# Five of eight sums over channels: added chunk by chunk on GpSimd, then one product with ones

## What is computed

```python
h = rms_norm_2(x, mix_norm)                    # mean of squares over the 1024 channels
a, g = split(h @ w_in + b_in)                  # conformer_conv
h = a * sigmoid(g)
h = causal depthwise convolution of 31 taps + conv_b
h = silu(layer_norm(h, ln_g, ln_b))            # mean, then mean of squares of the difference
x = x + (h @ w_out + b_out)
x = x + square(relu(rms_norm_2(x, mlp_norm) @ w1)) @ w2     # again a mean of squares
```

## Time and profile before

| | |
|---|---|
| median of three runs | 3348.47 us |
| the profiled execution: its own time | 3347.38 us |
| its span (first to last instruction) | 3345.6 us |
| PE busy | 3172.8 us, 95% |
| DVE busy | 2033.8 us, 61% |
| ACT busy | 1068.4 us, 32% |
| POOL busy | 315.4 us, 9% |
| share of PE in the chain that ended last | 78% |

### The profile page before, as it was taken

One profiled execution on the slowest core, in us unless ns is written; L12 is line 12 of the kernel. 1 busy time (PEld: TensorE's weight loads), 2 busy tenths in 40 slices (PEclk: granted clock), 3 DMA queues, 4 the chain that ended last, 5 costly groups with the idle time before them and its releaser, 6 DMA issues.

```text
span 3345.6 us, 52078 instructions
## 1 busy us (share of the span) xinstructions
PE 3172.8 (95%) x22004; PEld 2531.4 (76%) x22004; DVE 2033.8 (61%) x3235; ACT 1068.4 (32%) x1526; POOL 315.4 (9%) x307
## 2 busy tenths in 40 slices
PE   8999999788988888999999999999999999999999
PEld 7777786577766666778888888877746888778887
DVE  4665454577777775535444454448979987654445
ACT  5222334444444442222111111123244333433332
POOL 0222342000000000400000000000000000000000
PEclk9999999799999998999999999999999999999999
DMA  3342666234344433421111111111101222223222
GB/s 144 120 138 63 219 217 197 72 80 105 85 104 99 98 65 136 152 95 38 51 51 39 50 51 51 51 38 38 38 25 51 89 100 101 83 81 126 96 93 76
DMA packets 93527, 301.86 MB, mean 90 GB/s; under 512 B 10352, under 2 KB 38640, under 8 KB 70768
## 3 DMA queue, kind: packets, MB, share of 16 engines
q1 hardware_dynamic: 79104, 246.63, 23.7%
q0 software_dynamic: 14192, 51.91, 4.6%
HBM read 241.35 MB, written 57.15 MB: 89 GB/s over the span
## 4 chain that ended last, share of the span: by engine, by line
PE 78%; DVE 11%; DMA 3%; issue 3%; ACT 2%; POOL 2%; SPq 1%; DVEq 0%; ACTq 0%; POOLq 0%
PE ps L2416 26%; PE ps L308 20%; PE ps L503 6%; PE ps L1755 3%; PE ps L2239 2%; PE ps L2559 2%; DMA Dn<-nbs 2%; PE ps L2074 1%; DVE Yh L2586 1%; PE ps L475 1%; PE ps L1423 1%; PE ps L1766 1%; PE ps L1778 1%; PE ps L1019 1%; PE ps L2436 1%
## 5 line engine op out<-in xcount | busy, mean ns | idle before, releaser
L2416 PE MATMUL ps<-Hh,whi 128*128 128x512 f32 x1600 | 498.0, 393 | 0.6 <-DVE wlo L288 0.6
L284 ACT ACTIVATE whi<-raw 128x2048 fp32r<-128x2048 f32 x139 | 265.7, 1912 | 590.7 <-PE ps L308 290.6
L288 DVE TENSOR_TENSOR wlo<-raw,whi 128x2048 fp32r<-128x2048 f32 x139 | 319.0, 2295 | 136.8 <-ACT whi L284 136.6
L2416 PEld LDWEIGHTS ps<-Hh,whi 128*128 128x128 f32 x1600 | 300.2, 188 | 69.3 <-issue 5.7
L2416 PE MATMUL ps<-Hh,wlo 128*128 128x512 f32 x800 | 311.4, 389 | 0.0
L308 PE MATMUL ps<-Hlo,whi 128*128 128x512 f32 x656 | 202.0, 389 | 0.0
L308 PE MATMUL ps<-Hhi,wlo 128*128 128x512 f32 x656 | 202.0, 389 | 0.0
L308 PE MATMUL ps<-Hhi,whi 128*128 128x512 f32 x656 | 202.0, 389 | 0.0
L2416 PE MATMUL ps<-aHh,whi 128*128 128x512 f32 x512 | 199.4, 389 | 0.1
L2416 PE MATMUL ps<-aLh,whi 128*128 128x512 f32 x512 | 199.3, 389 | 0.0
L2416 PE MATMUL ps<-aHh,wlo 128*128 128x512 f32 x512 | 199.3, 389 | 0.0
(11 more groups left out here) (385 smaller groups left out, 6175.9 us busy)
## 6 DMA issues: line engine op xcount, KB each, us to landing
raw<-in_panels SPq DMA_DIRECT2D x139, 1024.0 KB, 4.8
rwf<-F POOLq DMA_DIRECT2D x16, 1280.0 KB, 6.8
L<-rwf SPq DMA_DIRECT2D x16, 1024.0 KB, 4.9
L<-rwf SPq DMA_DIRECT2D x64, 256.0 KB, 4.1
Dn<-nbs SPq DMA_DIRECT2D x128, 128.0 KB, 5.7
gts<-so POOLq DMA_DIRECT2D x16, 512.0 KB, 3.5
gl<-gts SPq DMA_DIRECT2D x32, 256.0 KB, 3.4
rwt<-so POOLq DMA_DIRECT2D x15, 512.0 KB, 3.0
```

The lines of the kernel that those rows point to most:

```text
L284: e.activation(whi[i % 2][:, :], raw_of(i)[:, :], AF.Copy).then_inc(*a_hi.up(i))
L288: e.tensor_tensor(wlo[i % 2][:, :], raw_of(i)[:, :], whi[i % 2][:, :].bitcast(F32), OP.subtract).then_inc(*v_lo.up(i))
L2416: m = e.matmul(ap, W[wi][:, kc, n0:n0 + 128], mov[mi][:, kc, :], start=x == 0 and q == 0, stop=x == len(kcs) - 1 and q == 2)
```

## The change

Five sums are made another way: `sum2` of both halves, and `mu`, `var` and `sum3` of half 1. The new `added_pool` adds the eight chunks on POOL, seven additions of 128 x 512 into `sgt[h]` (a buffer that is otherwise the sigmoid's); then PE makes one product of ones with `sgt[h]` (`added_pe`, or a line in `first_pe`). The other three sums (`mu`, `var`, `sum3` of half 0) stay as they are. ACT's squares wait for POOL's addition where they waited for PE's product. In `first_pe` the product stands behind the eight chunks and before the products of panel `ci1`. In `down_dve`, block 10, DVE now makes the low part of chunk n-1 after adding chunk n; before, it made chunks 0 and 1 there and the others behind the block. ACT makes all eight chunks of half 0 before the cast of panel `ci1`; before, that cast stood behind the fifth.

```diff
--- before.py
+++ after.py
@@ -2276,12 +2276,12 @@
 
     def down_dve(e, p, t, v, b):
         for n in range(8):
-            if b == 10 and n == 6:
-                first_lo_dve(e, 0, range(2))
             for h in range(2):
                 e.wait_ge(*t.by("x", b, n, h))
                 e.tensor_tensor(xT[:, n, hs(h)], ring.bank("down", p, n, h), xT[:, n, hs(h)],
                                 OP.add).then_inc(*v.up("x", b, n, h))
+            if b == 10 and n:
+                first_lo_dve(e, 0, range(n - 1, n))
         if b < 10:
             panels_after(panel_dve, e, p)
 
@@ -2426,6 +2426,25 @@
             made.append((ap, W, n0, key))
         return made
 
+    def added_pool(e, key, h, src_by, src, free=None):
+
+        for kc in range(1, 8):
+            if kc == 1:
+                if free:
+                    e.wait_ge(*free)
+                e.wait_ge(*src_by(0))
+            else:
+                e.wait_ge(*g_e.by(key, h, kc - 1))
+            e.wait_ge(*src_by(kc))
+            e.tensor_tensor(sgt[h], src(0) if kc == 1 else sgt[h], src(kc), OP.add).then_inc(*g_e.up(key, h, kc))
+
+    def added_pe(e, key, h):
+        ap, waits = ring.take((key, h), (v_e, key, h))
+        for w in waits:
+            e.wait_ge(*w)
+        e.wait_ge(*g_e.by(key, h, 7))
+        e.matmul(ap, ones, sgt[h], start=True, stop=True).then_inc(*t_e.up(key, h, 7))
+
     def sums_pe(e, key, src_by, src, kcs=range(8)):
         if kcs[0] == 0:
             ap, waits = ring.take(key, (v_e, *key))
@@ -2441,7 +2460,7 @@
         for kc in kcs:
             e.wait_ge(*v_ff.by("x", 10, kc, h))
             if kc >= 2:
-                e.wait_ge(*t_e.by("sum2", h, kc - 2))
+                e.wait_ge(*g_e.by("sum2", h, max(kc - 2, 1)))
             e.activation(tq[h][kc % 2], xT[:, kc, hs(h)], AF.Square).then_inc(*a_e.up("sq2", h, kc))
             if kc == 0:
                 e.wait_ge(*t_ff.by("u", 21, 1))
@@ -2474,8 +2493,6 @@
             e.wait_ge(*w)
         outs = outs_pe(e, [((x, h, 0), (v_e, x, h, 0), weights(p, 8), n0) for x, n0 in (("a", 0), ("gate", 128))])
         for kc in range(8):
-            e.wait_ge(*a_e.by("sq2", h, kc))
-            e.matmul(ap, ones, tq[h][kc % 2], start=kc == 0, stop=kc == 7).then_inc(*t_e.up("sum2", h, kc))
             e.wait_ge(*v_e.by("lo2", h, kc))
             for o, W, n0, key in outs:
                 for q, (wi, mi) in enumerate(THREE):
@@ -2483,6 +2500,8 @@
                                  stop=kc == 7 and q == 2)
                 if kc == 7:
                     m.then_inc(*t_e.up(*key))
+        e.wait_ge(*g_e.by("sum2", h, 7))
+        e.matmul(ap, ones, sgt[h], start=True, stop=True).then_inc(*t_e.up("sum2", h, 7))
         if h == 0:
             panel_pe(e, p + 1)
         for x, n0 in (("a", 0), ("gate", 128)):
@@ -2666,7 +2685,7 @@
                 for k in range(2):
                     half_pe(e, ("co", h, n + k), (v_e, "co", h, n + k), weights(i, 8), 128 * k, Gh[h], range(8))
             last_use[i] = (t_e, ("co", h, n + 1))
-            if n:
+            if n and h == 0:
                 sums_pe(e, ("sum3", h), lambda kc: a_e.by("sq3", h, kc), lambda kc: tl_[kc % 2], (n - 2, n - 1))
 
     def co_dve(e, h, n):
@@ -2680,7 +2699,7 @@
     def last_act(e, h, n):
         e.wait_ge(*v_e.by("co", h, n))
         if n >= 2:
-            e.wait_ge(*t_e.by("sum3", h, n - 2))
+            e.wait_ge(*(g_e.by("sum3", 1, max(n - 2, 1)) if h else t_e.by("sum3", 0, n - 2)))
         e.activation(tl_[n % 2], xT[:, n, hs(h)], AF.Square).then_inc(*a_e.up("sq3", h, n))
 
     def last_pe(e, h):
@@ -2726,7 +2745,7 @@
             for k in range(2):
                 half_pe(e, ("m", h, b, k), (a_e, "r", h, b, k), W, 128 * k, Gh[h], range(8))
                 if h == 0 and b == 15 and k == 0:
-                    last_pe(e, 1)
+                    added_pe(e, "sum3", 1)
         last_use[p] = (t_e, ("m", h, b, 1))
 
     def up_act(e, h, b):
@@ -2788,9 +2807,9 @@
             if b:
                 back_pe(e, 0, b - 1)
             if b == 12:
-                mean_pe(e, 1)
+                added_pe(e, "mu", 1)
             if b == 13:
-                var_pe(e, 1)
+                added_pe(e, "var", 1)
             if b == 14:
                 co_pe(e, 1)
         back_pe(e, 0, 15)
@@ -2804,9 +2823,8 @@
         done["B"] = 0
         for i, u in enumerate(uA):
             e.memset(u[:, 0:30], 0.0).then_inc(*v_e.up("pad", i))
-        first_lo_dve(e, 0, range(2, 5))
+        first_lo_dve(e, 0, range(7, 8))
         panels_after(panel_dve, e, UIX["fd10"])
-        first_lo_dve(e, 0, range(5, 8))
         mean_dve(e, ("sum2", 0), 0, 1e-6)
         first_lo_dve(e, 1, range(4))
         recip_dve(e, ("sum2", 0), 0)
@@ -2908,9 +2926,8 @@
             back_dve(e, 1, 15, n)
 
     def late_act(e):
-        first_act(e, 0, range(5))
+        first_act(e, 0)
         panels_after(panel_act, e, UIX["fd10"])
-        first_act(e, 0, range(5, 8))
         root_act(e, ("sum2", 0), 0)
         first_act(e, 1)
         root_act(e, ("sum2", 1), 1)
@@ -2981,8 +2998,13 @@
                 panels_after(panel_act, e, UIX[f"md{b - 1}'"])
 
     def late_pool(e):
+        for h in range(2):
+            added_pool(e, "sum2", h, lambda kc: a_e.by("sq2", h, kc), lambda kc: tq[h][kc % 2])
         for ch in range(8):
             tail_pool(e, ch)
+        added_pool(e, "mu", 1, lambda ch: v_e.by("taps", 1, ch), lambda ch: Yh[1][:, ch, :], last_tap(1, 7))
+        added_pool(e, "var", 1, lambda ch: a_e.by("sqy", 1, ch), lambda ch: sqy(1, ch), t_e.by("mu", 1, 7))
+        added_pool(e, "sum3", 1, lambda n: a_e.by("sq3", 1, n), lambda n: tl_[n % 2], t_e.by("var", 1, 7))
 
     def late_sp(e):
         panels_sp(e, UIX["mg0"] + 7, UIX["mu4'"])
```

## The result

The changed kernel takes 3326.32 us (median of four runs, 3316.74 to 3328.50) against 3350.61 for the kernel before on the same chips (four runs, 3344.15 to 3353.14). The ratio is 0.9925 with a 95% interval of 0.990 to 0.9949: 25 us faster, between 17 and 34. The forecast was 3321.9, a gain of 25.5; the median lies 4.4 us above it, and the two medians are 24.3 apart. The profiled execution has a span of 3324.4 us, 21.2 less than before.

The account below looks back on a forecast made before the run. PE, busy 95% of the span, was taken as the bound. A gross 30.5 us less waits of 0.7, 2.5 and 1.8 gave 25.5, so 3347.38 became 3321.9 us; range 3317 to 3327, 8 in 10 for 3313 to 3332.

Parts of the forecast that it names:

- The gross, 30.5 us: PE's work saved at the five sums: 12.4 us for both `sum2`, 12.0 for `mu` and `var`, 6.1 for `sum3`.
- POOL is never late: At `sum2`, `mu` and `sum3` POOL's additions, 1.27 us alone, 1.8 where DVE is dense, cost PE 0.
- Term 1: Behind `sum2` of half 1, PE waits about 0.7 us (0 to 1) for a bank that DVE reads.
- Term 2: Behind `mu`, POOL's `var` additions delay DVE's subtractions and panel `md12`'s low part; PE waits 2.5 us (0 to 5.9).
- Term 3: Behind `var`, PE reaches `co_pe` before DVE frees its bank and waits 1.8 us (0 to 2.5).
- POOL costs DVE more than one panel: Rival: the 21 additions of `sum2` and `mu` also block low parts and taps; gain 14 us, 3333; chance 0.15.
- The gross did not come through unreduced: Denies the rival that none of the three waits appears and the full 30.5 us comes: 3316.9 us; chance 0.20.
- The swallowed stage: Rival: the DVE-led stage of 2497 to 2578 swallows `sum2`'s 12.4 - 0.7 us: 3333.6; chance 0.06.
- Slower through long additions: Rival: POOL's addition far longer than 1.27 us, PE waits at the sums; slower from 4.4 us on; chance 0.02.
- the estimate by turns of 1.09: At panel `md12`: five POOL turns each cost DVE 1.09 us; low part 13.3 us after `mean_dve`, PE waits 2.5.
- the one by the full addition: At panel `md12`: by the exclusive port rule each turn costs DVE the full 1.27 us; PE waits 3.3.

Follow-up runs that it names:

- version 8: Changed kernel plus the edits of experiment 4, experiment 6 and experiment 7, and `sum2`'s product of ones of half 1 ahead of the last chunk's products: 3316.59 us.
- experiment 4: Changed kernel, but POOL waits for the last of the eight squares before its first addition of `var`: 3324.03 us, ratio 0.9941.
- experiment 7: On top of experiment 4, DVE reads the first two chunks of `back_pe(0, 13)` before making the first co panel's low part: 3316.66 us, ratio 0.991.
- experiment 1: Changed kernel with `var` of half 1 put back to eight products of ones on PE, no POOL additions for it: 3325.46 us, ratio 0.994.
- experiment 3: Kernel before, plus POOL's seven additions of `var`, half 1, whose sum nobody reads: 3354.17 us, ratio 1.0019.
- experiment 6: On top of experiment 4, DVE takes the mean of `var` ahead of the low part of panel `md13`: 3326.08 us, ratio 0.9935.
- experiment 2: Changed kernel with only the two sums `sum2` on POOL; `mu`, `var` and `sum3` of half 1 as before: 3342.03 us, ratio 0.9984.
- experiment 5: Changed kernel with the first half's low parts and ACT's cast of panel `ci1` back in their old order: 3331.00 us, ratio 0.9947.

## Why the prediction was right, point by point

- **The gross, 30.5 us: right.** From the ledger with the waits taken out: `sum2` 57.71 - 45.33 = 12.4 (version 8, without the bank's wait), `mu` and `var` 28.64 - 22.67 = 6.0 each (experiments 4 and 7), and `sum3` the 4.26 of the last row with the 1.88 of slower products taken out: 6.1 (experiment 1, which has no slower products there, takes 427.77 in that row). Together 30.5.
- **POOL is never late: right.** No wait of PE for POOL, in the changed kernel or with POOL later or PE sooner (4, 8). The size was right too: 1.29 alone against the 1.27 taken, 1.5 to 1.6 in company against 1.8. In `sum2` of half 1 ACT waited for POOL for 1.7 us in all, with cover.
- **Term 1, the bank behind `sum2`, 0.7: there, a little short.** The record of the wait is 0.7; the stretch without it is 1.06 shorter (46.39 against 45.33).
- **Term 2, panel `md12`, 2.5: right in place, mechanism and size.** Subtractions of 9.3 instead of 4.9, the low part 13.3 us behind `mean_dve` (2856.4 - 2843.08), a wait of 2.5. Experiment 3 makes it in the kernel before by additions alone, experiment 4 takes it away by their start alone.
- **Term 3, the bank ahead of `co_pe`, 1.8: right**, 1.9 recorded and 1.9 in the stretch (24.60 against 22.67). Experiments 1 and 7 take it away, by a later PE and by a sooner read; experiment 6 cuts it to 0.5 by a sooner mean.
- **What the sum left out.** By terms 1 to 3 as measured (1.06 + 2.5 + 1.9) the ledger should read -25.0, and it reads -19.6. Of the 5.4 us missing, 1.88 are slower products behind the wait of term 3 and 0.3 behind term 2: I priced a wait at its length, and it can cost as much again. 0.7 are `mu`'s additions against DVE in the feed-forward, up to `mu` apart from the first 48 products (261.84 against 261.12; 261.8 in all profiles with these additions, 261.12 in experiments 2 and 3 without them). At the first such addition one tap takes 1.68 us and not 0.76, and in the 25 us behind it PE's weight loads wait 0.9 us for line 288, where the kernel before has no wait. I had put that at 0, under the rival that POOL costs DVE more than one panel; it is there, at a thirtieth of the 23 us of DVE's time that this rival counted with. That count was too high as well: DVE is busy for 15.1 us more with all 35 additions, and for 4.1 more with the 14 of `sum2` alone (experiment 2), so many additions meet no instruction of DVE that they delay. The last 2.5 us lie at the seam of taps and `up_pe(0, 0)`, and nothing ties them to the change: 0.94 is one product of ones in 2.09 us and not 1.14, and experiments 1, 4, 5 and 8, with the same code there, have 1.14; the other 1.56 are the first 48 products of `up_pe(0, 0)`, 14.05 against 12.49, and experiment 3, whose code is up to there that of the kernel before, has 13.54.
- **The total agrees better than the ledger.** The measured 25 us against 25.5 owes something to chance, since a gain of 19.6 in the last part is what one execution of each kernel shows, and the interval reaches from 17 to 34.
- **The rivals.** The gross did not come through unreduced: three waits stand in the profile. The swallowed stage: no, the stretch from taps to up is 294.4 to 295.4 in every kernel. Slower through long additions: no, 1.29 us alone and 3.2 at most.

## What to carry to other kernels

When work leaves the engine that bounds, draw up what that engine then reaches sooner (a bank, a panel, a buffer) and by how much its maker moves. Ahead of `co_pe` the maker moved some 2.5 us where PE moved 6, and the difference, less the 1.6 us that the bank had been early, was the new wait. An idle GpSimd is not free beside a dense VectorE: let its additions of SBUF tiles run where VectorE reads PSUM or idles, as one wait more did here. And judge each moved piece alone: by the ledger four of the five sums gave all of the gain, and the fifth gave its share only with POOL's later start and DVE's sooner reads (experiment 7).

## What the runs showed of the hardware

- **Turns between DVE and POOL.** Eight subtractions of 0.6 us took 9.3 us beside additions of 1.29. The changed kernel's timeline has ACT's squares, each made from one subtraction, and POOL's additions:

```profile
2848.04 0.64 ACT L2644 ACTIVATE uB<-Yh 128x512 f32<-128x512 f32 x1 [1.06 <-DVE Yh L2637]
2849.74 0.63 ACT L2644 ACTIVATE uB<-Yh 128x512 f32<-128x512 f32 x1 [1.07 <-DVE Yh L2637]
...
2845.94 1.52 POOL L2439 TENSOR_TENSOR sgt<-uB,uB 128x512 f32<-128x512 f32 x1 [22.92 <-ACT uB L2644]
2847.54 11.72 POOL L2439 TENSOR_TENSOR sgt<-sgt,uB 128x512 f32<-128x512 f32 x6
```

  The squares go on at 2851.44 and 2853.14, 1.70 apart, which is one subtraction and one turn of 1.1 for POOL. POOL pays too: 1.29 became 3.2 when a panel's subtraction of 2.29 came first. The other five of POOL's six additions take 8.5 us, again 1.70 each. The Trainium skill states in SBUF — State Buffer, "Who interferes with whom", that a VectorE instruction with two inputs in SBUF contends with a GpSimd one that reads SBUF, and that the lock is exclusive. The runs agree with that: 1.1 us are lost for a turn of 1.29, so that the estimate by turns of 1.09 (13.3 us) came nearer than the one by the full addition (14.2). That the two alternate, one instruction each, is what the trace adds.
- **A short wait of PE can be followed by a low clock, or not.** Two stretches of 5 us in the changed kernel, the first behind the wait ahead of `co_pe`, the second behind the one ahead of `up_pe(0, 0)` (the granted clock is the third number from the end of a row):

```profile
2893.00:2898.00 5.00, 5.00 (x16) 3.96 (x15) 5.00 (x9) 2.12 (x2) 0.00 (x0) 0.66 0.27 113
2567.00:2572.00 5.00, 5.00 (x14) 3.84 (x13) 4.68 (x8) 2.48 (x4) 0.00 (x0) 0.50 0.00 0
```

and the second place in the kernel before, the end of the wait and what follows it:

```profile
2575.00:2580.00 5.00, 1.73 (x4) 1.47 (x5) 4.72 (x7) 1.89 (x3) 0.00 (x0) 0.77 0.35 147
2580.00:2585.00 5.00, 5.00 (x21) 4.00 (x21) 4.69 (x8) 2.06 (x4) 0.00 (x0) 0.89 0.00 0
```

  0.50 is the lower level, 1.2 GHz of 2.4; the numbers between 0.50 and 1.00 mix both. Behind waits of nearly one length the 48 products took 12.76 and 11.15 (1.9 us ahead of `co_pe`, changed kernel and experiment 4) or 11.18 and 12.78 (2.5 and 2.6 us for `md12`, changed kernel and experiment 3). Where they took 11.15 and 11.18 the granted clock is 1.00 all along, so the 0.3 us over 10.88 are not the clock's; where they took 12.76 and 12.78 it is 0.50 for two us or so. At `up_pe(0, 0)`, where every kernel idles some 4 us, they took 12.49 to 14.05 in ten profiles, without a pattern by what was changed. A little ahead of it stands the last product of ones of half 0's `sum3`: 2.09 us at a granted clock of 0.50 in the changed kernel, 1.14 at 1.00 in the kernel before. These two are the 2.5 us that the ledger has too much. When the clock falls and when not, these runs do not settle.
- **The spread lies ahead of the change.** Behind the end of block 10, stretches of like code repeat within 0.1 us, but for the clock just told; up to there, ten profiles differ by 16 us (2220.3 to 2236.2). Where in the first 2200 us that arises was not followed up.
